# The last contraction rows of the attention scores as two smaller products in different row groups

## What is computed

```python
    s = jnp.einsum('bqgrd,bkgd->bgrqk', qb, k_g, preferred_element_type=jnp.float32) * scale_g
    p = jax.nn.softmax(s, axis=-1).astype(v_g.dtype)
...
    s = (jnp.einsum('bqhd,bkhd->bhqk', qn, k_nope, preferred_element_type=jnp.float32)
         + jnp.einsum('bqhd,bkd->bhqk', qr, k_rope, preferred_element_type=jnp.float32)) * scale_m
    p = jax.nn.softmax(s, axis=-1).astype(v_m.dtype)
```

## Time and profile before

| | |
|---|---|
| median of 3 runs | 2997.29 us (2993.71 to 2999.22) |
| the profiled execution's own time | 2994.37 us |
| its span | 2992.6 us |
| mean granted TensorE clock | 0.972 of 2.4 GHz |
| PE, PEld busy | 94%, 88% of the span |
| DVE, ACT, POOL busy | 61%, 49%, 23% |
| L1388 scores | 379.0 us busy, 1392 products |
| DMA q1 (issued by SP) | 510256 packets, 411.74 MB |

### The profile page before, as it was taken

One profiled execution on the slowest core, in us unless ns is written; L12 is line 12 of the kernel. 1 busy time (PEld: TensorE's weight loads), 2 busy tenths in 40 slices (PEclk: granted clock), 3 DMA queues, 4 the chain that ended last, 5 costly groups with the idle time before them and its releaser, 6 DMA issues. The chain is left out here.

```text
span 2992.6 us, 56058 instructions
## 1 busy us (share of the span) xinstructions
PE 2826.5 (94%) x20084; PEld 2619.8 (88%) x20084; DVE 1820.7 (61%) x3158; ACT 1479.4 (49%) x2701; POOL 684.4 (23%) x1247
## 2 busy tenths in 40 slices
PE   8999899999999999999999999999965999999994
PEld 7888698999998888887999999988844999999994
DVE  6777767888887777676334334433345555555555
ACT  4333336888887777677223223321222445544443
POOL 0000013444443333334000000000013233332331
PEclk9999898999999999999999999999976999999997
DMA  6556592202113224443757564456655898889977
GB/s 212 158 157 191 152 377 86 71 24 72 50 33 93 75 74 108 102 125 99 225 137 228 160 203 132 144 174 197 190 138 141 198 207 199 201 203 209 207 161 260
DMA packets 529044, 461.87 MB, mean 154 GB/s; under 512 B 53458, under 2 KB 464802, under 8 KB 528880
## 3 DMA queue, kind: packets, MB, share of 16 engines
q1 hardware_dynamic: 510256, 411.74, 48.0%
q0 software_dynamic: 16256, 47.89, 7.5%
q10 hardware_dynamic: 2368, 0.16, 0.0%
HBM read 315.57 MB, written 144.14 MB: 154 GB/s over the span
## 5 line engine op out<-in xcount | busy, mean ns | idle before, releaser
L1576 DVE TENSOR_REDUCE t_peak<-t_s_ps 128x1 f32<-128x1024 f32 (+2 forms) x276 | 336.8, 1221 | 84.8 <-PE t_s_ps L1388 83.9
L1388 PE MATMUL t_s_ps<-t_k,t_q 96*128 96x512 f32 (+2 forms) x1392 | 379.0, 402 | 4.8 <-ACT t_probs L1492 4.8
L1840 PE MATMUL c_acc<-c_tokens,c_w_hi 128*128 128x260 f32 x2048 | 373.0, 283 | 4.5 <-DVE c_w_lo L1913 4.5
L1601 DVE TENSOR_TENSOR t_pt_lo<-t_tp,t_pt_hi 128x512 fp32r<-128x512 f32 x552 | 336.4, 650 | 36.1 <-ACT t_pt_hi L1522 35.5
L1522 ACT CAST t_pt_hi<-t_tp 128x512 fp32r<-128x512 f32 x552 | 284.7, 565 | 113.0 <-PE t_tp L1418 112.0
L1840 PEld LDWEIGHTS c_acc<-c_tokens,c_w_hi 128*128 128x128 f32 x2048 | 316.8, 189 | 4.8 <-issue 4.8
L1492 ACT ACTIVATE t_probs<-t_s_ps,t_bias 128x1024 f32<-128x1024 f32 (+2 forms) x276 | 308.2, 1117 | 22.8 <-POOL t_bias L1655 8.1
L2445 PE MATMUL e_gu<-e_x_hi,w_hi 128*128 128x260 f32 x1024 | 293.7, 287 | 0.9 <-DVE e_x_lo L2650 0.9
L2445 PE MATMUL e_gu<-e_x_lo,w_hi 128*128 128x260 f32 x1024 | 289.9, 283 | 0.0
L1840 PE MATMUL c_acc<-c_tokens,c_w_lo 128*128 128x260 f32 x1024 | 289.8, 283 | 0.0
L2445 PE MATMUL e_gu<-e_x_hi,w_lo 128*128 128x260 f32 x1024 | 289.6, 283 | 0.0
(11 more groups left out here) (299 smaller groups left out, 6569.2 us busy)
## 6 DMA issues: line engine op xcount, KB each, us to landing
c_raw<-in_w_in SPq DMA_DIRECT2D x64, 512.0 KB, 5.6
w_raw<-in_w_gate SPq DMA_DIRECT2D x64, 512.0 KB, 6.9
w_raw<-in_w_up SPq DMA_DIRECT2D x64, 512.0 KB, 9.3
w_raw<-in_w_down SPq DMA_DIRECT2D x64, 512.0 KB, 4.5
c_tokens<-o_t SPq DMA_DIRECT2D x32, 520.0 KB, 6.7
c_tokens<-hn_t SPq DMA_DIRECT2D x16, 1040.0 KB, 9.3
r_mt<-mix_t SPq DMA_DIRECT2D x32, 512.0 KB, 5.2
mix_t<-c_out_hi SPq DMA_DIRECT2D x32, 260.0 KB, 2.1
```

The lines of the kernel that those rows point to most:

```text
L1388: ins = pe.matmul(s_ps[0:r, n % 2, half * 512:(half + 1) * 512], query(n, a), key(n, c, half * 512, (half + 1) * 512), start=(at == 0), st ...
L1576: dve.tensor_reduce(peak[0:r, b % 2, i:i + 1], s_ps[0:r, n % 2, :], AX_X, ALU.max).then_inc(peak_done, 1)
L1601: dve.tensor_tensor(pt_lo[span], tp[:, f % RING, :].rearrange("p (t n) -> p t n", t=4)[:, :, 0:r], pt_hi[span].bitcast(F32), ALU.subtract) ...
L1840: pe.matmul(acc[:, b, mixer, 0:W], w[:, parity, mixer, k, :], tokens[t % 2][:, part, k, cols], start=(k == 0 and at == 0), stop=(k == DK - ...
```

## The change

With grouped heads the pass that multiplied all 128 query rows by the low keys (where only the 64 high query rows carry a term that is kept) becomes two products of 64 rows: queries in partitions 0 to 63 for the first 512 keys, and for the other 512 keys a copy of the same queries in partitions 64 to 127. SP makes that copy (`raised`, four buffers) block by block, two blocks ahead. The products of the low query rows with the low keys are left out with it.

With latent heads the 288 contraction rows of the three passes are stacked anew: two passes of 128 rows, and 32 rows left, which become two products of 32 rows for half of the keys each, in partitions 32 to 63 and 64 to 95. The loads fill the stacked tiles, with rows repeated: 26 transfers in place of 14. The meta scores take one product of 128 rows and one of 64.

```diff
     def load_qk(self, sp, scr, u):
...
+            def put(tile, x, meta):
+                sp.dma_start(tile[:, 0:SEQ].bitcast(F32).rearrange("p (i n) -> p i n", n=2 * P), x.rearrange("i p n -> p i n"))\
+                    .then_inc(loaded, 16)
+                sp.dma_start(tile[:, SEQ:TOK].bitcast(F32), meta).then_inc(loaded, 16)
...
+            one, two, three = (q[:, i * TOK:(i + 1) * TOK] for i in range(3))
+            for stacked in (one, two):
+                put_straight(stacked[0:NOPE, :], 0, 0, nope)
+                put_rotated(stacked[rotated, :], 0)
+            put_rotated(one[extra, :], 1)
+            put_straight(two[extra, :], 1, 0, low)
+            put_straight(three[0:NOPE, :], 1, 0, nope)
+            put_straight(three[rotated, :], 1, 0, high)
             for part in range(2):
...
+                put_straight(k[0:NOPE, p, part, :], part, 1, nope)
+                sp.dma_start(k[rotated, p, part, :].bitcast(F32), scr["kr_t"][part, g, :, :]).then_inc(loaded, 16)
+            sp.dma_start(k[extra, p, 0, :].bitcast(F32), scr["kr_t"][0, g, :, :]).then_inc(loaded, 16)
+            sp.dma_start(k[extra, p, 1, 0:SEQ].bitcast(F32).rearrange("p (i n) -> p i n", n=2 * P),
+                         scr["mqk_x"][0, g, :, low, 1, h // 2, :].rearrange("i p n -> p i n")).then_inc(loaded, 16)
+
+            sp.dma_start(k[extra, p, 1, SEQ:TOK].bitcast(F32), self.v[NOPE:QK_M, p, XCH, 0:META].bitcast(F32)).then_inc(loaded, 16)
+            sp.dma_start(self.far_keys(p)[:, :].bitcast(F32).rearrange("p (i n) -> p i n", n=2 * P),
+                         scr["mqk_x"][0, g, DOUBLES // 2:, high, 1, h // 2, :].rearrange("i p n -> p i n")).then_inc(loaded, 16)
...
+            def raise_queries(b):
+
+                if b >= BLOCKS or units[unit_of(b)][0]:
+                    return
+                u = unit_of(b)
+                at = chunks[b * PER][1]
+                sp.wait_ge(qk_loaded[u % 2], qk_after[u])
+                if b >= RAISED:
+                    sp.wait_ge(s_filled, (b - RAISED + 1) * PER)
+                sp.dma_start(raised[HD:P, b % RAISED, 0:width(b)].bitcast(F32), q[u % 2][0:HD, at:at + width(b)].bitcast(F32))\
+                    .then_inc(raised_loaded[b % RAISED], 16)
+
             last_unit = first_block[len(units) - 1]
             for b in range(BLOCKS):
                 u = unit_of(b)
                 starts = first_block[u] == b and u + 1 < len(units)
+                if b == 0:
+                    raise_queries(0)
+                    raise_queries(1)
                 if starts:
                     load_qk(u + 1)
+                raise_queries(b + 2)
                 if b > 0:
                     store(b - 1)
...
+            def by_halves(n):
+
+                (u, at, r), b, i = chunks[n], n // PER, n % PER
+                if i == 0:
+                    pe.wait_ge(raised_loaded[b % RAISED], 16 * (b // RAISED + 1))
+                pe.matmul(s_ps[0:r, n % 2, 0:512], q[u % 2][0:HD, at:at + r], k[0:HD, u % 2, 1, 0:512], start=False, stop=True)
+                return pe.matmul(s_ps[0:r, n % 2, 512:SEQ], raised[HD:P, b % RAISED, i * P:i * P + r],
+                                 k[HD:P, u % 2, 1, 512:SEQ], start=False, stop=True)
...
+                mla, p = units[chunks[n][0]][0], chunks[n][0] % 2
+                for at in range(2 if mla else 1):
                     for half in range(2):
...
+                        pe.matmul(s_ps[0:r, n % 2, half * 512:(half + 1) * 512], query(n, at),
+                                  key(n, at, half * 512, (half + 1) * 512), start=(at == 0), stop=False)
+                if mla:
+
+                    pe.matmul(s_ps[0:r, n % 2, 0:512], remainder(n, ROT, NOPE), k[ROT:NOPE, p, 0, 0:512], start=False, stop=True)
+                    ins = pe.matmul(s_ps[0:r, n % 2, 512:SEQ], remainder(n, NOPE, QK_M), held.far_keys(p), start=False, stop=True)
+                else:
+                    ins = by_halves(n)
                 ins.then_inc(s_filled, 1)
...
                     if mla:
-                        ins = pe.matmul(out[:, 0:META], query(n, 1), key(n, 0, SEQ, TOK), start=False, stop=True)
+                        ins = pe.matmul(out[:, 0:META], remainder(n, 0, NOPE), k[0:NOPE, u % 2, 0, SEQ:TOK], start=False, stop=True)
```

More of the change, by code:

```diff
@@ L171, in __init__, with far_keys @@
         self.v_loaded = [nc.alloc_semaphore("t_v_loaded0"), nc.alloc_semaphore("t_v_loaded1")]
+    def far_keys(self, p):
+        return self.q[p][NOPE:QK_M, 3 * TOK:3 * TOK + SEQ // 2]
     def load_qk(self, sp, scr, u):
@@ L177, in load_qk @@
         if mla:
-            half = slice(h % 2 * NOPE, h % 2 * NOPE + NOPE)
-            turned = slice(h % 4 * ROT, h % 4 * ROT + ROT)
-            for part in range(2):
[L181 to L190, removed]
@@ new lines, in load_qk @@
+            first = h % 2 * NOPE
+            nope, low, high = slice(first, first + NOPE), slice(first, first + ROT), slice(first + ROT, first + NOPE)
+            turned, rotated = slice(h % 4 * ROT, h % 4 * ROT + ROT), slice(NOPE, QK_M)
+            extra = slice(QK_M, P)
+            def put(tile, x, meta):
+                sp.dma_start(tile[:, 0:SEQ].bitcast(F32).rearrange("p (i n) -> p i n", n=2 * P), x.rearrange("i p n -> p i n"))\
+                    .then_inc(loaded, 16)
+                sp.dma_start(tile[:, SEQ:TOK].bitcast(F32), meta).then_inc(loaded, 16)
@@ new lines, in put_straight, with put_rotated @@
+            def put_straight(tile, part, which, rows):
+                put(tile, scr["mqk_x"][part, g, :, rows, which, h // 2, :], scr["mqk_meta"][part, rows, which, h // 2, :])
+            def put_rotated(tile, part):
+                put(tile, scr["mrot_x"][part, g, :, turned, h // 4, :], scr["mrot_meta"][part, turned, h // 4, :])
+            one, two, three = (q[:, i * TOK:(i + 1) * TOK] for i in range(3))
+            for stacked in (one, two):
+                put_straight(stacked[0:NOPE, :], 0, 0, nope)
+                put_rotated(stacked[rotated, :], 0)
@@ L1164, in attention @@
     PAIR = M_AT + META
+    RAISED = 4
     units = UNITS
@@ L1235, in attention @@
         pt_hi, pt_lo = sb("pt_hi", [P, 2, XCH, WIDE], F32R), sb("pt_lo", [P, 2, XCH, WIDE], F32R)
+        raised = sb("raised", [P, RAISED, WIDE], F32R)
         s_ps = ctx.enter_context(nc.psum_tensor("t_s_ps", [P, 2, SEQ], F32))
@@ L1240, in attention @@
         qk_loaded, v_loaded = held.qk_loaded, held.v_loaded
+        raised_loaded = [sem(f"raised_loaded{k}") for k in range(RAISED)]
         stored = [sem("stored0"), sem("stored1")]
@@ L1255, in attention @@
         for u, (mla, _, _) in enumerate(units):
-            qk_total[u % 2] += 16 * (14 if mla else 4)
+            qk_total[u % 2] += 16 * (26 if mla else 4)
             v_total[u % 2] += 16 * 3
@@ L1362, in query, with remainder @@
                 u, at, r = chunks[n]
-                if units[u][0]:
-                    return q[u % 2][0:QK_M, part * TOK + at:part * TOK + at + r]
-                return q[u % 2][:, at:at + r]
+                return q[u % 2][:, part * TOK + at:part * TOK + at + r]
             def key(n, part, lo, hi):
                 u = chunks[n][0]
-                return k[0:QK_M if units[u][0] else P, u % 2, part, lo:hi]
-            def passes(n):
-                return [(0, 0), (0, 1), (1, 0)] if units[chunks[n][0]][0] else [(0, 0), (0, 1)]
+                return k[:, u % 2, part, lo:hi]
+            def remainder(n, lo, hi):
+                u, at, r = chunks[n]
+                return q[u % 2][lo:hi, 2 * TOK + at:2 * TOK + at + r]
+            def by_halves(n):
[5 more added lines that the diff above has]
+                                 k[HD:P, u % 2, 1, 512:SEQ], start=False, stop=True)
             def loaded_before(n):
@@ L1384, in scores @@
                     pe.wait_ge(exp_done, n - 1)
-                todo = passes(n)
-                for at, (a, c) in enumerate(todo):
+                mla, p = units[chunks[n][0]][0], chunks[n][0] % 2
+                for at in range(2 if mla else 1):
                     for half in range(2):
-                        ins = pe.matmul(s_ps[0:r, n % 2, half * 512:(half + 1) * 512], query(n, a),
-                                        key(n, c, half * 512, (half + 1) * 512),
-                                        start=(at == 0), stop=(at == len(todo) - 1))
+                        pe.matmul(s_ps[0:r, n % 2, half * 512:(half + 1) * 512], query(n, at),
[5 more added lines that the diff above has]
+                    ins = by_halves(n)
                 ins.then_inc(s_filled, 1)
@@ L1402, in meta_scores @@
                     mla = units[u][0]
-                    both = k[0:QK_M if mla else P, u % 2, :, SEQ:TOK]
+                    both = k[:, u % 2, :, SEQ:TOK]
                     out = tp[0:rows(n), f % RING, i * 2 * META:(i + 1) * 2 * META]
```

## The result

The changed kernel takes **3249.82 us** (median of 4 runs, 3245.29 to 3250.6), beside 2996.65 for the kernel before on the same chip: a ratio of **1.084 (95% interval 1.082 to 1.086)**, 253 us more. The forecast was 3218, in a range from 3140 to 3270. The profiled execution of it took 3249.49 us, its span is 3247.7, and the mean granted clock fell from 0.972 to 0.942 of 2.4 GHz.

What follows compares the result with a forecast made beforehand. The prediction took PE (TensorE), 94% busy and full in the attention stage, as the bound. Grouped heads +80 and latent heads +142 made 222 us on the profiled 2994.4: 3217, stated from the median as 3218, range 3140 to 3270.

Steps and rivals of the forecast that it cites:

- The bound: Attention stage: PE is busy 99.6 to 100 of 100 us, so work taken from it shows if nothing arrives late.
- PE, s = 0.233 - 0.18 = +0.05 us: Score products: each chunk saves 0.233 us, pays 0.18 for two row changes; 14 us gained over 276 chunks by itself.
- The bounds of 0.23 and -0.23: Score products, gain per chunk: 0.23 us if no change costs, -0.23 with no overlap and both changes paid in full.
- Meta products, 0.4 us per latent block: Latent heads: one of each pair becomes a 64-row product, six row changes, costing 0.4 us per block (none to 0.6).
- Grouped heads, +80: Raised copies land late behind loads and stores: losses of 44.4, 29.4 and 9 us, less 2.6, sum +80 us.
- The ordinary blocks: Grouped heads, 26 blocks away from unit starts: copy slightly late, yet scores shorter, -2.6 us in all.
- Latent heads, +142: Latent load of 26 transfers lands at 17.9 us, not 10.8; fourteen loops of 42.95 us add 132.5, +142 in all.
- The clock: PE after long stalls: clock falls to the 1.2 GHz level, costing 2.9 us each time.
- the second rival, that the clock holds: PE after stalls: stays at 2.4 GHz or stalls are short enough, 61 us less, 3156; chance 0.15.
- Faster (1): SP's queue: SP keeps ahead and only PE's shorter work counts, 2930 with the full 0.233; chance 0.04.
- Early copies (3): Grouped heads: copies get past the big loads and nothing is lost, only the latent loop counts, 3123; chance 0.10.
- No overlap (4): Score products: the last two run one after the other, both row changes paid, -0.23 us per chunk, 3284; chance 0.10.

Runs made afterwards that it cites:

- fifth: Changed kernel with raised copies and unit loads issued earlier, plus each chunk's half-height pair issued twice: 3094.57 us, ratio 1.034.
- sixth kernel: Changed kernel with raised copies and unit loads issued earlier, plus both halves of each pair in the same row group: 3095.05 us, ratio 1.034.
- third kernel: Changed kernel with raised copies issued three blocks ahead instead of two, in front of the next unit's load: 3176.82 us, ratio 1.061.
- ninth kernel: Kernel before, with only the load of each unit's keys and queries issued one block earlier: 2979.04 us, ratio 0.9957.

## Why the prediction was right, point by point

The loss came by the mechanism that was summed: late transfers and the lower clock behind them are 218.5 us, some 204 of them more than in the kernel before, of a loss of 253. PE's own term had the wrong sign; the time stayed in the range because that term is small beside the waits.

- **The bound.** Right: the loss shows as idle PE and lower clock, in both stretches.
- **PE, s = 0.233 - 0.18 = +0.05 us.** This is the term that was mis-sized. It is -0.10 in the mean and about -0.12 in an ordinary chunk: the overlap is whole (the fifth and sixth kernel), but the changes cost 0.33 to 0.35, not 0.18. The earlier trace rows were the right place to look, a 16-row weight load that starts after 0.20 us of idle, but they showed one change whose way back cost 0.03; the pair stalls the weights both ways, 0.36 and 0.24 us. The working also charged all 276 chunks alike, and the last chunk of a latent unit gains 0.46. The bounds of 0.23 and -0.23 held it. The Trainium skill (TensorEngine Tiling, Key Properties) says that a change of tiling mode drains TensorE: the traces agree, with idle weight loads at each change, and they price it. In 276 chunks the error is 276 x 0.15 = 41 us where nothing hides it, and some of it hides under the waits; the total missed by 32.
- **Meta products, 0.4 us per latent block.** Measured 24.7 / 48 = 0.51.
- **Grouped heads, +80.** The grouped part alone costs 89, and another 7 fall on it where the first latent load of 26 stands in its last unit. The stalls were 8.69 and 7.50 us (9.3 and 7.1 predicted), the longest 16.4 (16.5). The ordinary blocks don't gain 0.1 each but lose 0.4 (three medians of 0.11, 0.13 and 0.16), 0.5 more in 26 blocks, 13 us.
- **Latent heads, +142.** The latent part alone costs 154. PE goes on 17.3 us after the first issue (17.9), the next load starts 24.7 after that (24.5 - 5 x 0.05 + 0.8 = 25.05 by the working), 42.0 in that loop against 42.95. But the mean of the 14 is 43.6, 141 us over before in place of 132.5: thirteen took 42.3 to 44.6 us, and one, with a wait of 9.61, 47.3. With s = -0.10 the same working gives 24.5 + 0.5 + 0.8 + 17.9 = 43.7.
- **The clock.** 2.9 us behind each long wait, from one case in the earlier trace rows, is also the mean over the 16 of the third kernel, and the clock fell to 0.50 at every one of them. So the second rival, that the clock holds, fell.
- **The other rivals.** Faster (1): SP did not keep ahead, 0.58 us per transfer (14.5 / 25). Early copies (3): they were not, at the unit starts. No overlap (4): the overlap is there (a drain at a change of height, which the prediction names as this rival's mechanism, would explain the paid changes, not halves in turn), but its sign of s was right, and that is the larger part of why the time came out above the forecast.

In one account: 218.5 us of late transfers, 24.7 for the meta products' and 27.6 for the pairs' changes of rows make 270.8 over the ninth kernel; less the 14.5 that the kernel before loses against that one, 256. These are steps from one kernel to the next, so they add up by construction, and the 3 us to the measured 253 are the kernel before on two chips (2996.65 and 2993.58). What bears the account out are the counted waits and the pitches at the pair.

## What to carry to other kernels

Two half-height products side by side cost one product, but the way into and out of their row group, between products of full height, cost more than that saves. A pair should pay where the changes are shared. Two pairs in a row, each for one product less, would gain 2 x 0.233 - 0.35 = 0.12 us: an estimate from the fifth kernel, in which a further pair cost one product and no change; no such kernel was run. What the traces do show is the pair ahead of 16-row transposes, where it gained 0.46. Count the transfers that a new operand layout adds on the one queue that issues them, and read from the timeline when the last of them would land against when it is needed; a wait that is a few tenths long now is a sign that a later landing would show in full. And a queue in program order is worth a look by itself: here a load issued one block earlier gained 14.5 us with no product touched.

## What the hardware showed that was not expected

- The price of a row change depends on the neighbours. A pair between full-height products lost 0.11 to 0.12 us a chunk; ahead of transposes of 16 rows, which started within 4 ns of it, it gained 0.46. Of the 15 us that the pair cost when it was put ahead of the full products, 8 are this place lost.
- Even a product of 16 columns pays 0.10 us for a neighbour of another height (0.21 in place of 0.11).
